# Decode stage of a hybrid decoder step: where key pages are turned, how scans and value pages are split, and in which order two loads and two buffers stand

## The reference, cut to what matters

```python
def sample_prepare(k, v, logf, past_k, past_v, past_logf):
    k_all = jnp.concatenate([past_k.astype(k.dtype), k], axis=1)       # 256 cached keys + 4 new
    v_all = jnp.concatenate([past_v.astype(v.dtype), v], axis=1)
    c_all = jnp.cumsum(jnp.concatenate([past_logf, logf], axis=1), axis=1)

s = jnp.einsum('nqhd,nkhd->nhqk', q, k) * (HEAD_DIM ** -0.5)
s = s + (c_q[..., :, None] - c_k[..., None, :])                        # forget term, causal mask
p = jax.nn.softmax(s, axis=-1)
y = jnp.einsum('nhqk,nkhd->nqhd', p, v)                                # then y @ w_o
```

## Time and profile before

| what | value |
|---|---|
| time before, median of 3 runs (lowest, highest) | 2576.71 us (2576.52, 2578.64) |
| the profiled execution's own time, its span | 2579.46 us, 2577.3 us |
| PE busy, share of the span | 2532.1 us, 98% |
| PEld, DVE, ACT, POOL busy | 96%, 70%, 41%, 1% |
| mean granted clock of TensorE | 0.996 |
| last group of the prompt's attention ends | 1694.8 us from the span's start |
| the woven stage (eight units of w_o) | 1695.8 to about 1848 us |
| PE waits for DVE k_t_lo (L1330) in the whole program | 7.9 us, 11 times, longest 3.0 |
| a step of a unit, six matmuls of 358 columns, at clock 1.00 | 0.99 us |
| a quarter of keys turned, four transposes, at clock 1.00 | 0.43 us |
| fourth key quarter turned at, sequences 1 to 7 (starts on PE, L1300) | 1722.20, 1740.14, 1756.96, 1773.80, 1790.52, 1807.27, 1824.02 us |
| value copy by ACT (L1438), 128x2048 | 1900 ns |
| weight copy by ACT (L567), 128x1024 | 1050 ns |
| a half of the result kept by ACT (L1468), 64x512 | 587 ns |

### The profile page before, as it was taken

One profiled execution on the slowest core, in us unless ns is written; L12 is line 12 of the kernel. 1 busy time (PEld: TensorE's weight loads), 2 busy tenths in 40 slices (PEclk: granted clock), 3 DMA queues, 4 the chain that ended last, 5 costly groups with the idle time before them and its releaser, 6 DMA issues.

```text
span 2577.3 us, 45916 instructions
## 1 busy us (share of the span) xinstructions
PE 2532.1 (98%) x18332; PEld 2478.4 (96%) x18332; DVE 1809.4 (70%) x2437; ACT 1049.1 (41%) x1491; POOL 24.4 (1%) x48
## 2 busy tenths in 40 slices
PE   8999999999999999999999999989999999999998
PEld 7999999999999999999999899978899999999998
DVE  5444437667788998944345898876597666889986
ACT  3111124333333232465245777755563333333233
POOL 0000000000000000000000100000000000000000
PEclk9999999999999999999999999999999999999999
DMA  4111111322353312024325556533323322533111
GB/s 119 49 42 42 48 42 40 123 100 100 104 193 119 116 66 86 19 86 156 111 77 157 135 143 149 135 126 130 100 87 100 104 100 100 184 134 131 54 51 68
DMA packets 248431, 259.43 MB, mean 101 GB/s; under 512 B 18161, under 2 KB 182961, under 8 KB 248291
## 3 DMA queue, kind: packets, MB, share of 16 engines
q1 hardware_dynamic: 229030, 248.37, 30.9%
q10 hardware_dynamic: 19260, 9.09, 1.2%
HBM read 193.86 MB, written 63.42 MB: 100 GB/s over the span
## 4 chain that ended last, share of the span: by engine, by line
PE 91%; DVE 3%; ACT 2%; issue 1%; DMA 1%; ACTq 0%; SPq 0%; DVEq 0%
PE ps L591 28%; PE ps L790 24%; PE ps L845 23%; PE ps L1252 2%; PE ps L1167 1%; PE ps L810 1%; PE ps L1102 1%; PE ps L1253 1%; PE ps L1254 1%; PE ps L1169 1%; PE ps L1458 1%; PE ps L1300 1%; PE ps L692 1%; PE ps L629 1%; DMA tokens_in<-in_x_prompt 0%
## 5 line engine op out<-in xcount | busy, mean ns | idle before, releaser
L845 PE MATMUL ps<-h_op,w_op 128*128 128x268 f32 x4912 | 615.4, 287 | 2.7 <-DVE w_op L885 2.5
L845 PEld LDWEIGHTS ps<-h_op,w_op 128*128 128x128 f32 x4912 | 610.9, 189 | 3.4 <-DVE w_op L885 3.4
L591 PE MATMUL ps<-x_hi,w_hi 128*128 128x358 f32 x1248 | 277.3, 330 | 4.5 <-DVE w_lo L575 4.5
L575 DVE TENSOR_TENSOR w_lo<-w_raw,w_hi 128x1024 fp32r<-128x1024 f32 x76 | 92.8, 1221 | 257.5 <-ACT w_hi L567 257.5
L591 PE MATMUL ps<-x_hi,w_lo 128*128 128x358 f32 x1248 | 273.5, 327 | 0.0
L591 PE MATMUL ps<-x_lo,w_hi 128*128 128x358 f32 x1248 | 273.3, 327 | 0.0
L856 ACT ACTIVATE w_op<-w_op_f 128x2048 fp32r<-128x2048 f32 (+1 forms) x54 | 97.6, 1808 | 388.6 <-PE ps L845 367.7
L591 PEld LDWEIGHTS ps<-x_hi,w_hi 128*128 128x128 f32 x1248 | 213.8, 190 | 6.4 <-DVE w_lo L575 4.9
L591 PEld LDWEIGHTS ps<-x_lo,w_hi 128*128 128x128 f32 x1248 | 216.2, 189 | 0.0
L591 PEld LDWEIGHTS ps<-x_hi,w_lo 128*128 128x128 f32 x1248 | 215.8, 189 | 0.0
L1040 DVE TENSOR_TENSOR t<-ps,t 128x536 f32<-128x536 f32 x180 | 128.7, 715 | 120.2 <-PE ps L790 111.3
(11 more groups left out here) (358 smaller groups left out, 5183.7 us busy)
## 6 DMA issues: line engine op xcount, KB each, us to landing
raw_a<-in_mlp_w SPq DMA_DIRECT2D x120, 256.0 KB, 3.0
h_op_f<-h_rows SPq DMA_DIRECT2D x24, 1072.0 KB, 6.5
w_op_f<-in_mlp_w SPq DMA_DIRECT2D x24, 1024.0 KB, 7.5
h_rows<-t SPq DMA_DIRECT2D x90, 268.0 KB, 2.1
w_raw<-in_conv_w_in SPq DMA_DIRECT2D x24, 512.0 KB, 3.7
w_raw<-in_w_kv SPq DMA_DIRECT2D x16, 512.0 KB, 4.8
w_raw<-in_w_o SPq DMA_DIRECT2D x16, 512.0 KB, 4.0
k_page<-in_cache_k SPq DMA_DIRECT2D x16, 512.0 KB, 4.8
```

The costliest lines, as they stand in the source:

```text
L575: dve.tensor_tensor(WL[:, s], RAW[:, s], WH[:, s].bitcast(F32), ALU.subtract).then_inc(w_lo, 1)
L591: mm = pe.matmul(PS[:, bank(s, g), 0:GW], w[:, s, k], x[:, k, g * GW:(g + 1) * GW], start=(k == 0 and n == 0), stop=(k == KC - 1 and n == 2))
L845: mm = pe.matmul(PS[:, 2 * p + g, 0:QW], w[:, k, P * m:P * m + P], x[:, k, QW * g:QW * g + QW], start=(k == 0 and j == 0), stop=(k == tile ...
```

## The change

It edits the tables and the orders; no product is left out or added.

1. Keys are turned at p = 0, 2, 4, 5 in slot 0 and p = 0, 2, 4 in the others; the fourth quarter of sequence n is turned at p = 4 between the two halves of the value product of sequence n - 1.
2. `past_scan` takes one sequence: sequence 0 in group 4 of the last head, 1 in slot 1 behind `d_probs_lo`, n + 1 at the end of slot n.
3. `d_values_lo` of sequence 0 is made a page at a time, with a key subtraction between; `dv_lo` counts pages. The new values and the value pages of sequence 0 are split ahead of tile 7 on ACT.
4. SP issues v_new and the value pages of sequence 0 ahead of `load_inverse` of the last head.
5. VD stands ahead of v_page_lo, away from the inverse, and v_new still lies on v_page_lo.
6. In slot 0, ACT and DVE split the first key quarter ahead of tile 3 and of the new keys, and the queries directly behind it.

```diff
-TURN_AT = [{1: 0, 2: 1, 3: 2, 4: 3}] + [{0: 0, 2: 1, 3: 2, 4: 3}] * (DB - 1)
+TURN_AT = [{0: 0, 2: 1, 4: 2, 5: 3}] + [{0: 0, 2: 1, 4: 2}] * (DB - 1)
...
         VPH = put("v_page_hi", [P, NPAGE, D], F32R)
+        VD = put("v_new_hi_hi_lo", [3 * NS, D], F32R)
         VN, _ = place("v_new", [3 * NS, D], offset=decode_end[0])
         VPL = put("v_page_lo", [P, NPAGE, D], F32R)
-        VD = put("v_new_hi_hi_lo", [3 * NS, D], F32R)
...
+        def d_values_lo(b, g=None):
             dve.wait_ge(dv_hi, b + 1)
             dve.wait_ge(vn_lo, 1)
+            pages = slice(0, NPAGE) if g is None else slice(g, g + 1)
+            dve.tensor_tensor(VPL[:, pages, :], VPG[:, pages, :], VPH[:, pages, :].bitcast(F32), ALU.subtract)\
+               .then_inc(dv_lo, NPAGE if g is None else 1)
...
+        def d_weigh(b, h):
+            if h == 0:
+                if b == 0:
+                    pe.wait_ge(acc_free, 3 * HEADS)
+                    pe.wait_ge(vn_lo, 1)
+                pe.wait_ge(dv_lo, NPAGE * (b + 1))
+                pe.wait_ge(dp_used, 2 * b + 2)
+                ge(pe, dw_kept, 2 * b)
+            f = slice(512 * h, 512 * h + 512)
...
             def load_v_pages(b):
-                ge(sp, dv_lo, b)
+                ge(sp, dv_lo, NPAGE * b)
...
                 spread_sums(HEADS - 1)
-                load_inverse(HEADS - 1)
                 sp.wait_ge(pv_done, NG * HEADS)
                 for x in range(3):
                     sp.dma_start(VN[NS * x:NS * x + NS, :], out["v_sample"].rearrange("b t h d -> (b t) (h d)"))\
                       .then_inc(vn_loaded, 16)
                 load_v_pages(0)
+                load_inverse(HEADS - 1)
                 load_o(2)
...
+            act.wait_ge(pv_done, NG * HEADS)
+            d_keys_hi(0, 0)
+            o_split_hi(3)
             act.activation(KTH[:, :, PAST:KEYS], KSS[:, :, :], ACT.Copy).then_inc(kn_hi, 1)
-            for x in range(4):
+            d_queries_hi(0)
+            for x in range(1, 4):
                 d_keys_hi(0, x)
                 o_split_hi(3 + x)
-            d_queries_hi(0)
+            act.wait_ge(vn_loaded, 48)
+            act.activation(VD[:, :], VN[:, :], ACT.Copy).then_inc(vn_hi, 1)
+            d_values_hi(0)
             act.wait_ge(kn_lo, 1)
             o_split_hi(KC - 1)
             d_cross(0)
             d_keys_hi(1, 0)
             d_exp(0)
-            act.wait_ge(vn_loaded, 48)
-            act.activation(VD[:, :], VN[:, :], ACT.Copy).then_inc(vn_hi, 1)
-            d_values_hi(0)
+            d_keys_hi(1, 1)
...
                 if h == HEADS - 1:
                     if g == 1:
                         mask_rows()
-                    if 4 <= g < 7:
-                        past_scan(range(2 * g - 8, 2 * g - 6))
+                    if g == 4:
+                        past_scan(0)
...
+            d_keys_lo(0, 0)
+            o_split_lo(3)
             dve.wait_ge(kn_hi, 1)
             dve.tensor_tensor(KTL[:, :, PAST:KEYS], KSS[:, :, :], KTH[:, :, PAST:KEYS].bitcast(F32),
                               ALU.subtract).then_inc(kn_lo, 1)
-            for x in range(4):
+            d_queries_lo(0)
+            invert_sums(HEADS - 1)
+            for x in range(1, 4):
                 d_keys_lo(0, x)
                 o_split_lo(3 + x)
-                if x == 1:
-                    invert_sums(HEADS - 1)
-            d_queries_lo(0)
             divide(HEADS - 2)
             divide(HEADS - 1)
+            dve.wait_ge(vn_hi, 1)
+            low = VD[2 * NS:3 * NS, :]
+            dve.tensor_tensor(low, VN[2 * NS:3 * NS, :], low.bitcast(F32), ALU.subtract).then_inc(vn_lo, 1)
             o_split_lo(KC - 1)
             d_max(0)
             d_keys_lo(1, 0)
             d_norm(0)
-            dve.wait_ge(vn_hi, 1)
-            low = VD[2 * NS:3 * NS, :]
-            dve.tensor_tensor(low, VN[2 * NS:3 * NS, :], low.bitcast(F32), ALU.subtract).then_inc(vn_lo, 1)
-            d_values_lo(0)
+            d_values_lo(0, 0)
+            d_keys_lo(1, 1)
+            d_values_lo(0, 1)
             for n in range(1, DB):
-                d_keys_lo(n, 1)
+                if n > 1:
+                    d_keys_lo(n, 1)
                 d_probs_lo(n - 1)
+                if n == 1:
+                    past_scan(1)
                 d_keys_lo(n, 2)
                 d_keys_lo(n, 3)
...
-                if n == 1:
-                    past_scan(range(6, DB))
+                if n < DB - 1:
+                    past_scan(n + 1)
...
                 if p == 4 and 1 <= n <= DB:
-                    d_weigh(n - 1)
+                    d_weigh(n - 1, 0)
+                    if n < DB:
+                        d_turn_keys(n, 3)
+                    d_weigh(n - 1, 1)
```

More of the change, by code:

```diff
@@ L1438, in d_values_hi @@
             act.activation(VPH[:, :, :], VPG[:, :, :], ACT.Copy).then_inc(dv_hi, 1)
-        def d_values_lo(b):
+        def d_values_lo(b, g=None):
             dve.wait_ge(dv_hi, b + 1)
             dve.wait_ge(vn_lo, 1)
[L1444 to L1461, removed]
+            pages = slice(0, NPAGE) if g is None else slice(g, g + 1)
[10 more added lines that the diff above has]
+            f = slice(512 * h, 512 * h + 512)
+            for g in range(NPAGE):
+                for n in range(3):
+                    pe.matmul(PS[0:HQ, D_OUT + h, :], (DPL if n == 1 else DPH)[:, g], (VPL if n == 2 else VPH)[:, g, f],
+                              start=(g == 0 and n == 0), stop=False)
+            pe.matmul(PS[0:HQ, D_OUT + h, :], DPH[0:3 * NS, NPAGE], VD[:, f], start=False, stop=True).then_inc(dw_done, 1)
         def d_keep(b):
@@ L1778, in attention_scalar @@
             d_exp(0)
-            act.wait_ge(vn_loaded, 48)
-            act.activation(VD[:, :], VN[:, :], ACT.Copy).then_inc(vn_hi, 1)
-            d_values_hi(0)
+            d_keys_hi(1, 1)
             for n in range(1, DB):
-                d_keys_hi(n, 1)
+                if n > 1:
+                    d_keys_hi(n, 1)
                 d_probs_hi(n - 1)
@@ L1940, in mask_rows, with past_scan @@
                 dve.tensor_copy(MB[:, b, DQ * b:DQ * b + DQ], M4[:, :]).then_inc(d_mask, 1)
-        def past_scan(seqs):
+        def past_scan(b):
             dve.wait_ge(past_kept, 6)
-            for b in seqs:
-                dve.tensor_tensor_scan(CS[:, b], heads1[0:NH, 0:1].bitcast(F32).to_broadcast([NH, KEYS]), CS[:, b],
-                                       0.0, ALU.mult, ALU.add).then_inc(d_sums, 1)
+            dve.tensor_tensor_scan(CS[:, b], heads1[0:NH, 0:1].bitcast(F32).to_broadcast([NH, KEYS]), CS[:, b],
+                                   0.0, ALU.mult, ALU.add).then_inc(d_sums, 1)
         def add_prompt(n):
```

## The result

| | before | changed |
|---|---|---|
| median of 4 runs each | 2577.68 us | 2564.43 us |
| lowest, highest | 2576.52, 2580.65 | 2564.02, 2567.34 |
| ratio of the runs | | 0.9949, 95% interval 0.9937 to 0.9961 |
| profiled execution, span | 2579.46, 2577.3 | 2564.02, 2561.7 |

By the ratio the change saves 10 to 16 us; forecast were 12.7, from 2576.71 to 2564.0. A second set of 5 runs gave 2564.49 and a ratio of 0.9947 (0.9933 to 0.9960).

What follows compares the result with a forecast made beforehand. PE was taken to bound the kernel, its waits due to the order of DVE's queue. Up to the first value product 8.7, slots 4.6, less edges 0.6: 12.7 us, from 2576.71 to 2564.0 us; range 2560.5 to 2569.5.

Steps and rivals of the forecast that it cites:

- Part 1: Last head: moving scans out shortens PE's waits by 1.5 us; scans reappearing in slots are costed at nothing.
- Part 2: Slot 0, attention's end to first logits: logits at about 1701.9, 6.8 us earlier, with 2.8 for the clock.
- Part 3: Load queue, pages ahead of inverse: inverse lands at 1704, tile 7 gains 5.1 us, PE waits 1.6 there.
- Part 4: First value product: DVE's queue of 6.1 us after tile 7, start at 1713.9, 8.7 us gained up to here.
- Part 5: Steady slots: with key turns spaced, waits go and periods fall to about 16.1 us, gaining 4.6 us.
- the edges of 0.6: Later slots: 0.6 us taken off for work made late by the moved key quarter, bounds 0 and 2.
- The edge at the kept halves: Later slots: ACT keeps two output halves after the moved quarter's work, done within a tenth of PE's 1.98 us.
- the risk: Rival: clock falls all the same in slot 0, some 2 us lost, 2566 us; chance 0.14.
- The inverse is late: Rival: inverse lands at its upper bound behind the pages, 2.2 us more, 2566.2 us; chance 0.12.
- The other three: Rivals: even spacing gives nothing, 2567 us, chance 0.12; slower, 2585, 0.03; nearly nothing changes, 2572, 0.06.

Runs made afterwards that it cites:

- scans_only: Kernel before the change with only the scans moved, out of the last head into the slots: median 2574.32 us, ratio 0.9985.
- scans_turns: Kernel before the change with the scans moved and the key turns spaced, nothing else: median 2566.57 us, ratio 0.9952.
- turns_only: Kernel before the change with only the key turns of sequences 1 to 7 spaced, the fourth inside the value product: median 2571.73 us, ratio 0.9971.
- scans_back: Changed kernel with three pairs of scans back in the last head and the last pair in slot 1: median 2565.93 us, ratio 0.9950.
- tile_first: Changed kernel with the inverse issued between new values and value pages, and ACT's pages' copy behind tile 7, cross term and key quarter: 2561.43 us, ratio 0.9936.
- both: tile_first with weights ahead of the values in slot 5 and their subtraction behind the scaling in slot 6: median 2563.70 us.
- best: tile_first with the first value pages copied one by one around exp, and the weights' subtraction behind the scaling in slots 5 and 6: median 2564.46 us.
- final: best with only slot 6's move of the weights' subtraction kept: median 2563.38 us, ratio 0.9939.
- changed_again: The changed kernel unedited, run again with 5 runs: median 2564.49 us, ratio 0.9947 against the kernel before.

## Why the prediction was right, and where a step was not

**The sum.** 12.7 were forecast, 12.0 and 10.6 are in the two traces of the stage, and the medians give 13.3 twice. All lie inside the range. That the sum came so near is in part luck: the first value product gained 1.3 less than I had put, and the slots 0.6 more. That the first profiled pair differs by 15.4 is for the most part a start that was 3.1 us earlier, which no step of mine had.

**Part 1** gave 1.8 for 1.5. That the scans cost nothing in their slots held with the spacing, and not without it (scans_only, scans_turns): in slots 2 to 4 the argument stood on the right condition.

**Part 2** put the first logits at 1701.9; they came at 1702.2 on the old scale, 6.6 gained for 6.8. The clock stayed at 1.00 here in all eleven traces without the idle time, and fell in two of the three that have it (before and turns_only, not scans_back). What it is worth is less sure than the 2.8 that I took: scans_only gains 4.7 at the logits, 1.7 at the attention's end and 0.99 at the first tile, which leaves 2.0 for the clock, net of one more wait of 0.4 at a key turn.

**Part 3 is the step that failed by size.** I took the inverse to land at 1704, between bounds of 1702.3 and 1706.2. The division that waits for it starts at 1702.84, on the old scale 1705.9: 1.9 later, near the upper bound. Of this, 0.9 is that the store was issued at 1695.33, on the old scale 1698.4, where I had 1697.5; the rest is that from store to load it took 4.1 us behind the pages, where my 1704 left 3.0. So the rule of the Trainium skill that spoke against this move (DMA: Bandwidth & Descriptors, "Queues, rings and completion order"), that descriptors on one queue start in order, fits the trace, and my guess that the packets would be mostly through did not. Tile 7 gained 3.7 for 5.1, with a wait of 2.73 for 1.6.

**Part 4** carries this on: 7.4 for 8.7. The rest of its queue was sized right, 5.9 us from tile to product for 6.1; I had PE waiting 1 us there, and it waited 0.3. A split page took 1.21, twice that is 0.13 more than 2.29.

**Part 5** gave 4.6, and the edges of 0.6 are inside it: periods of 16.0 for 16.1, waits for probabilities of 0.21 and 0.49 in slots 5 and 6 for "about 0.3". The edge at the kept halves cost nothing.

**The rivals.** The clock was 1.00 in the first trace, and 0.50 for between 3 and 4 us in the second, at tile 7 and not at the attention's end. I had the risk, but in the wrong place: no step priced the clock behind a wait that the change itself makes. "The inverse is late" came true for the most part, 1.9 of its 2.2, and part 5 paid some of it back. The other three did not come.

## What to carry to other kernels

A queue entry is priced by when its follower is next asked for: by the traces the scans cost 0.5 us in each of three slots until the turns were spaced, and next to nothing then. But before two edits are called worth more together than apart, look at the granted clock of every trace: of a surplus of 4.6 us in single traces, 3.5 was a clock that happened to fall in the two single edits, and the medians showed no surplus. When a load moves ahead of another, look at every queue that waits for either: an early inverse made PE wait 5.92 us at tile 7 while ACT's order stood as it was, and 0.81 with the tile's copy ahead of the pages' and the inverse between the new values and the pages. And before a producer is moved to where its consumer has slack, ask which load waits for it too (4.4 us in one slot here).

## What the runs showed of the hardware

The granted clock after a short idle stretch is not the same from run to run of one kernel. Short stretches kept it at 1.00 or took it to 0.50: in the changed kernel 2.73 us of waiting kept it and 2.90 lost it, the value wait kept it at 3.01 (before) and 2.01 (scans_turns) and lost it at 2.99 (scans_only) and 2.00 (turns_only), and the old idle time at the attention's end lost it in two traces (before, turns_only) and kept it in one (scans_back), where an earlier stretch had lost it. Over 44 executions of the kernel before, its mean is 0.994 to 0.997, and time and clock go together (correlation -0.77): the medians are 2577.0 at 0.997 and 2579.4 at 0.995. It is 0.996 in the median before, 0.997 or 0.998 in most others, and 0.999 for tile_first and both, where the wait at tile 7 is 0.8; best and final have the same short wait and 0.998 and 0.997. The Trainium skill (TensorE: Matmul & The Clock Gate, "What's actually happening") has the slow clock as the default that activity releases; that rule leaves room for such a scatter, and what decides a single case no run here shows. For kernels like this one I take it that an idle stretch of 1 to 3 us on PE can have a second price, 1.1 to 1.9 us in the four traces where it can be read (changed_again, scans_back, turns_only, scans_only), paid in some executions and not in others.
